# A two-block transformer on one core: tensor work moved across five attention seams, fewer convolution taps at a stage's end, and two norm factors taken at other strips

## The reference, cut to what matters

```
for l in range(2):                       # first block
    h = rms_norm(x, norm_g[l]);  proj = h @ w_in[l]
    q, k_c, v_c, k_s, v_s, k_w, v_w, g, z_nsa, u_lru, z_lru, glu_a, glu_b, z_conv = split(proj)
    y_nsa  = three attentions (compressed, selected, window), 8 heads, 2 kv heads, gated
    y_lru  = gated linear recurrence over a 4-tap convolution of u_lru
    y_conv = silu(layer_norm(dwconv31(glu_a * sigmoid(glu_b)))) @ w_pw2
    x = x + concat(y_nsa*silu(z_nsa), y_lru*silu(z_lru), y_conv*silu(z_conv)) @ w_out[l]
x = rms_norm(x, final_g)
for l in range(2):                       # second block
    h2 = rms_norm(x, ...)
    # l = 0: dense attention with normed and rotated heads, and window attention with a sink
    # l = 1: latent attention (w_uq, w_ukv), and neighbourhood attention on an 8 x 64 grid
    x = x + mixed @ w_out2
    m = rms_norm(mem, g_mem[l]);  k, v = split(m @ w_xkv[l])
    q = rms_norm(x, g3[l]) @ w_xq[l]
    x = x + cross_attention(q, k, v) @ w_xo[l]          # 4 heads of 128, 256 keys
    g, u = split(rms_norm(x, g4[l]) @ w_gate_up[l]);  x = x + (silu(g) * u) @ w_down[l]
out = rms_norm(x, final_g_2)
```

## Time and profile before

| | |
|---|---|
| median of 3 runs | 2329.72 us (2325.25 to 2330.05) |
| the profiled execution's own time | 2332.14 us |
| its span | 2330.3 us |
| PE busy | 2206.3 us, 95% |
| DVE / ACT / POOL busy | 1261.5 / 1088.9 / 867.2 us |
| mean granted TensorE clock | 0.976 of full |
| DMA | 187 MB, mean 80 GB/s |

### The profile page before, as it was taken

The page is one execution under the profiler, slowest core; times in us unless marked ns, Lnnn a source line. Parts: engine busy times, 40 slices in busy tenths (PEclk is TensorE's granted clock), DMA queues, the critical chain, the costliest instruction groups (busy, mean ns, idle before and its releaser), DMA issues.

```text
span 2330.3 us, 33123 instructions
## 1 busy us (share of the span) xinstructions
PE 2206.3 (95%) x12030; PEld 1783.9 (77%) x12030; DVE 1261.5 (54%) x2638; ACT 1088.9 (47%) x2178; POOL 867.2 (37%) x681
## 2 busy tenths in 40 slices
PE   7999889999989999889899999999879989999997
PEld 6788667887866788668788888888648878888886
DVE  5987782488778446885552112234677455221222
ACT  6642474564247542685453223333557545332332
POOL 4433204443330343004255555544130424554553
PEclk9999899999989999999999999999999999999999
DMA  4324003333400232003233333342110323333332
GB/s 160 90 90 141 15 2 86 100 91 90 138 22 6 87 96 73 28 12 101 66 96 95 96 108 99 94 129 74 41 44 28 92 81 87 100 93 101 96 94 69
DMA packets 105551, 186.96 MB, mean 80 GB/s; under 512 B 11440, under 2 KB 22704, under 8 KB 105264
## 3 DMA queue, kind: packets, MB, share of 16 engines
q1 hardware_dynamic: 99504, 175.91, 25.7%
q10 hardware_dynamic: 5888, 8.95, 1.2%
HBM read 182.71 MB, written 2.10 MB: 79 GB/s over the span
## 4 chain that ended last, share of the span: by engine, by line
PE 82%; DVE 11%; ACT 3%; issue 3%; POOL 1%; DMA 1%; SPq 0%; DVEq 0%; ACTq 0%
PE bank L801 22%; PE bank L803 22%; PE bank L802 22%; PE bank L1002 3%; PE bank L990 3%; PE bank L1015 3%; DVE temp L1816 2%; PE bank L910 1%; DVE temp L1848 1%; DVE bank L1932 1%; DVE op_lo L1464 1%; POOL w_lo L2100 1%; PE bank L862 1%; DVE temp L1850 1%; DVE conv_area L1473 1%
## 5 line engine op out<-in xcount | busy, mean ns | idle before, releaser
L2100 POOL TENSOR_TENSOR w_lo<-w_raw,w_hi 128x512 fp32r<-128x512 f32 (+2 forms) x620 | 821.1, 1330 | 1356.1 <-ACT w_hi L1120 1355.6
L801 PE MATMUL bank<-op_hi,w_hi 128*128 128x512 f32 x1840 | 733.4, 399 | 14.6 <-DVE op_lo L1464 9.5
L1120 ACT ACTIVATE w_hi<-w_raw 128x512 fp32r<-128x512 f32 (+2 forms) x636 | 385.8, 615 | 719.1 <-PE bank L803 714.3
L803 PE MATMUL bank<-op_hi,w_lo 128*128 128x512 f32 x1840 | 718.9, 391 | 0.0
L802 PE MATMUL bank<-op_lo,w_hi 128*128 128x512 f32 x1840 | 718.6, 391 | 0.0
L801 PEld LDWEIGHTS bank<-op_hi,w_hi 128*128 128x128 f32 x1840 | 346.8, 189 | 97.7 <-issue 12.0
L802 PEld LDWEIGHTS bank<-op_lo,w_hi 128*128 128x128 f32 x1840 | 347.0, 189 | 76.3 <-issue 5.7
L803 PEld LDWEIGHTS bank<-op_hi,w_lo 128*128 128x128 f32 x1840 | 346.5, 188 | 73.5
L1534 DVE TENSOR_TENSOR temp<-bank,rstd 128x512 f32<-128x512 f32 (+1 forms) x151 | 104.4, 691 | 410.7 <-PE bank L803 401.6
L801 PE MATMUL bank<-side_hi,w_hi 128*128 128x512 f32 (+2 forms) x632 | 238.8, 378 | 3.7 <-DVE side_lo L1464 2.9
L1603 DVE TENSOR_TENSOR x_t<-bank,x_t 128x512 f32<-128x512 f32 x80 | 55.3, 692 | 342.1 <-PE bank L803 342.0
(11 more groups left out here) (256 smaller groups left out, 2298.9 us busy)
## 6 DMA issues: line engine op xcount, KB each, us to landing
w_raw<-in_weights SPq DMA_DIRECT2D x618, 256.0 KB, 2.7
w_raw<-in_weights SPq DMA_DIRECT2D x34, 192.0 KB, 2.3
x_t<-in_x SPq DMA_DIRECT2D x8, 256.0 KB, 5.6
conv_area<-in_mem ACTq DMA_DIRECT2D x2, 1024.0 KB, 5.7
out_y<-ybuf SPq DMA_DIRECT2D x8, 256.0 KB, 2.1
conv_area<-in_bias ACTq DMA_DIRECT2D x1, 1920.0 KB, 7.9
conv_area<-in_bias ACTq DMA_DIRECT2D x2, 960.0 KB, 6.0
temp<-in_lru_w ACTq DMA_DIRECT2D x2, 512.0 KB, 8.9
```

Source lines behind the costliest of these rows:

```text
L801: pe.matmul(dst, w[0], m[0], start=start, stop=False)
L803: return pe.matmul(dst, w[1], m[0], start=False, stop=stop)
L1120: act.activation(w_hi[:, j, 0:m * w], w_raw[:, p % RAW_RING, 0:m * w], ACT.Copy).then_inc(*mark("weights_high", p))
L2100: pool.tensor_tensor(w_lo[:, j, 0:n], w_raw[:, p % RAW_RING, 0:n], w_hi[:, j, 0:n].bitcast(F32), ALU.subtract).then_inc(*mark("weights_spl ...
```

## The change

1. **Taps.** A's table has 8 more in all (the first glu_a strip 6 instead of 4, the three others 8 instead of 6), B's last two entries go from 6, 6 to 4, 0. The total is 124 as before.
2. **Order of AB.** Before: keys and queries of the rotated heads, those of the normed heads, then both value strips. Now kn, qn x4, v, kr, qr x4, v. `UNITS`, the list of the rotations, is sorted to suit.
3. **Factors.** Two chunks of the memory are split and squared with each of OUT2's first four strips. `mem` is summed in OUT2's strip 6 and spread before strip 7. `h3` is summed before the last strip of XV and spread before chunk 6 of the first XQ strip.
4. **Drain.** `strip` is a generator that yields after each chunk. `drain` issues chunks of the next part's first two strips inside the last four steps of an attention, by the table `DRAIN` (0 and 1 are the two strips; a tuple for each step, the fourth after the last values). Their first matmul also waits until DVE has read the scores that the bank held. ACT and DVE split the second strip's weights ahead too.

```diff
-TAPS = {"A": [0, 0, 0, 4, 5] + 3 * [1, 2, 6, 6, 4],
+TAPS = {"A": [0, 0, 0, 6, 5] + 3 * [1, 2, 6, 8, 4],
...
-            for m in (1, 0):
+            for m in range(2):
                 base = 768 * m
                 add(("AB", 0), "kn" if m == 0 else "kr", 0, "w_in_ab_2", 0, base + 512, DC, ("h2", l))
                 for c in range(4):
                     add(("AB", 0), "qn" if m == 0 else "qr", c, "w_in_ab_2", 0, base + P * c, DC, ("h2", l))
-            for m in range(2):
-                add(("AB", 0), "v", m, "w_in_ab_2", 0, 768 * m + 640, DC, ("h2", l))
+                add(("AB", 0), "v", m, "w_in_ab_2", 0, base + 640, DC, ("h2", l))
...
-        for s in STRIPS:
+        for s in sorted(STRIPS, key=lambda s: (s.n + 3, 1) if s.kind in ("qn", "kn") else (s.n + 1, 0)):
...
-            if part[0] == "XV":
-                FACTOR_STRIP[name] = (rng[1], 0), (rng[2], 6), rng[2]
-            elif part[0] == "XK" or part == ("A", 0):
+            if part[0] == "OUT2":
+                FACTOR_STRIP[name] = (rng[6], 0), (rng[7], 0), rng[6]
+            elif part[0] == "XQ":
+                FACTOR_STRIP[name] = (rng[0] - 1, 0), (rng[0], 6), rng[0]
+            elif part == ("A", 0):
...
+        DRAIN = {"NSA": ((), (), (0, 0), (0, 0, 1, 1, 1, 1)),
...
+                 "X2": ((), (), (0, 0, 1, 1), ())}
...
+            def strip(n, fresh, between, held=None):
+
                 s = STRIPS[n]
+                if held is not None:
+
+                    pe.wait_ge(*after("maxed", held))
...
-                    ins.then_inc(*mark("weights_used", p))
+                        if k == k0 + m - 1:
+                            ins.then_inc(*mark("weights_used", p))
+                        yield k
...
+            def drain(part, steps):
+
+                first = FOLLOWS[part]
+                for r in steps:
+                    n = first + r
+                    if n not in begun:
+                        held = [t["a"] for t in ATT[part] if t["bank"] == n % 2]
+                        begun[n] = strip(n, True, {}, held[-1])
+                    next(begun[n])
...
                         if s < len(pairs):
                             scores(pairs[s])
+                        if len(pairs) <= s < len(pairs) + 3:
+                            drain(part, steps[s - len(pairs)])
...
+                drain(part, steps[3])
...
-                        strip(n, STRIPS[n].operand not in seen, between)
+                        for _ in begun.pop(n, None) or strip(n, STRIPS[n].operand not in seen, between):
+                            pass
...
-                    if s.part[0] == "OUT2":
...
+                    if s.part[0] == "OUT2" and s.idx < DC // 2:
...
+                        for c in (2 * s.idx, 2 * s.idx + 1):
+                            high(("mem", l), c, mem_t[:, c, :], PR("g_mem", l, c))
+                            square(("mem", l), c, mem_t[:, c, :])
...
-                        split_to(last_of(FOLLOWS[part]))
+                        split_to(last_of(FOLLOWS[part] + 1))
```

More of the change, by code:

```diff
@@ L60 @@
 SUMS = 24
-TAPS = {"A": [0, 0, 0, 4, 5] + 3 * [1, 2, 6, 6, 4],
-        "B": [1, 0, 4, 3, 0, 5, 0, 0, 0, 2, 0, 6, 2, 6, 0, 3, 3, 5, 6, 6, 6]}
+TAPS = {"A": [0, 0, 0, 6, 5] + 3 * [1, 2, 6, 8, 4],
+        "B": [1, 0, 4, 3, 0, 5, 0, 0, 0, 2, 0, 6, 2, 6, 0, 3, 3, 5, 6, 4, 0]}
 COLS = dict(zip(
@@ L497, in build @@
         for l in range(LAYERS):
-            FACTOR.update({("A", l): ("h1", l), ("AB", 0) if l == 0 else ("DN", 0): ("h2", l), ("XK", l): ("mem", l),
-                           ("XV", l): ("h3", l), ("FF", l, 0): ("h4", l)})
+            FACTOR.update({("A", l): ("h1", l), ("AB", 0) if l == 0 else ("DN", 0): ("h2", l), ("OUT2", l): ("mem", l),
+                           ("XQ", l): ("h3", l), ("FF", l, 0): ("h4", l)})
         FACTOR_STRIP = {}
@@ L833, in first_spread @@
                 ins.then_inc(*mark("first_spread", 0))
-            def strip(n, fresh, between):
+            def strip(n, fresh, between, held=None):
                 s = STRIPS[n]
+                if held is not None:
+                    pe.wait_ge(*after("maxed", held))
                 if n >= 2:
@@ L958, in later @@
                     rotate(n)
+            begun = {}
+            def drain(part, steps):
[6 more added lines that the diff above has]
+                    next(begun[n])
             def attend(part):
                 ts, between = ATT[part], extras(part)
+                steps = DRAIN[part[0]]
                 def scores(pair):
@@ L1211, in evac @@
                     square(s.stat, s.idx, x_t[:, s.idx, :])
-                    if s.part[0] == "OUT2":
-                        l, c = s.part[1], s.idx
-                        if c == 0:
+                    if s.part[0] == "OUT2" and s.idx < DC // 2:
+                        l = s.part[1]
+                        if s.idx == 0:
                             act.wait_ge(*after("mem_in", l))
-                        high(("mem", l), c, mem_t[:, c, :], PR("g_mem", l, c))
-                        square(("mem", l), c, mem_t[:, c, :])
+                        for c in (2 * s.idx, 2 * s.idx + 1):
+                            high(("mem", l), c, mem_t[:, c, :], PR("g_mem", l, c))
+                            square(("mem", l), c, mem_t[:, c, :])
                 elif k == "cmp2" and s.idx == 0:
@@ L1673, in side @@
                     add_squares(s.stat, s.idx)
-                    if s.part[0] == "OUT2":
+                    if s.part[0] == "OUT2" and s.idx < DC // 2:
                         name = ("mem", s.part[1])
-                        low(name, s.idx, mem_t[:, s.idx, :], PR("g_mem", s.part[1], s.idx))
-                        add_squares(name, s.idx)
+                        for c in (2 * s.idx, 2 * s.idx + 1):
+                            low(name, c, mem_t[:, c, :], PR("g_mem", s.part[1], c))
+                            add_squares(name, c)
                 if n in TURNS:
```

11 lines of the change are left out of this document (6 added, 5 removed).

## The result

The changed kernel took 2316.24 us (median of 4 runs, 2313.19 to 2317.5), the kernel before 2329.12 beside it: a ratio of 0.9937 (95% interval 0.9923 to 0.9950), which is 14.7 us (12.9 between the medians). Built and run a second time it took 2318.82, a ratio of 0.9947 (0.9927 to 0.9968). The forecast was 2300 and a range of 2288 to 2312: the sign was right and half of the gain was missing.

What follows compares the result with a forecast made beforehand. PE was taken as the bound, busy 2206.3 of 2330.3 us. The terms sum to -29.8: 2332.1 profiled gives 2302.3, and the median, 2.4 lower, 2300. Own range 2296 to 2305; with the first three rivals 2288 to 2312.

Steps and rivals of the forecast that it cites:

- Taps: At both NSA starts PE begins 4.0 us earlier without trailing taps, -8.0; a wait in layer 0's A costs 1.2: -6.8.
- -1.5 for the clock behind the NSA starts: After the NSA starts, shorter idle should shorten PE's 11 us at clock 0.50: -1.5 in all, bounds 0 and -5.
- the 1.2 that I gave for A: In layer 0's A the added taps make PE wait for DVE once, +1.2 us, bounds 0 and 3.6.
- Factors: XK and XV take 26.5 us, 27.9 with costs moved elsewhere, in place of 35.8: -7.9 a layer, -15.8.
- The first rival: In XK and XV, DVE and POOL exclude each other wholly: 31.6 us a stage, 5.1 more each, 2310; chance 18%.
- my argument against it in the prediction: In XK and XV, at 1095.6 to 1101.6, PE was 5.97 of 6.00 us busy with DVE and POOL both at work.
- Order of AB: At AB2's start PE's idle falls from 6.8 to 4.0 us: -2.8, bounds -5.4 and +1 if DVE falls behind.
- Drains: Early chunks fill idle PE in attention tails: AB2 -1.8, C2 -0.9, D2 -0.5, NSA -2.3; X2 instead loses 2.6.
- +2.6 for X2: In the cross attentions' tails nothing covers the copy, high and low parts: +1.3 a layer, bounds -0.5 and +2.5 each.
- X2's +0.9 for the values behind twelve matmuls: In X2's tail the last values wait behind twelve matmuls, about 2.1 us idle follow, and strip 1 ends 0.9 later.
- The second rival: In the attention tails the drains bring nothing and only reorder; gains of 5.5 are gone: 2306; chance 12%.
- The fourth: Rival: the clock falls at XK's start and stays low, +12.4 a layer, 2357 if through XQ; chance 4%.

Runs made afterwards that it cites:

- k2: The kernel before with only the new taps and factors (old order of AB, no chunks in attentions, no early split): 2306.65 us, ratio 0.9893.
- j4: The changed kernel without any chunk inside an attention and without any early split of a second strip's weights: 2307.07 us, ratio 0.9901 to before.
- b1: The kernel before with the new table of taps alone: 2317.82 us, ratio 0.9958.
- b2: The kernel before with the memory's split, its factor and h3's factor at the new places alone: 2317.41 us, ratio 0.9948.
- e3: The changed kernel with the memory's split, its factor and that of h3 at their old places: 2332.39 us, ratio 1.0008 to before.
- b4: The kernel before with the new order of AB alone: 2330.26 us, ratio 1.0006.
- e2: The changed kernel with the old order of the AB strips and of the rotations: 2316.73 us, ratio 0.9944 to before.
- e4: The changed kernel without any chunk inside an attention, the second strip's weights still split ahead: 2312.95 us, ratio 0.9919 to before.
- b3: The kernel before with the chunks inside the attentions and the early split alone: 2341.44 us, ratio 1.0049.
- j2: The kernel before with chunks and early split of the second strip's weights in the two cross attentions (X2) alone: 2339.04 us, ratio 1.0037.

## Why the prediction was wrong, step by step

Medians: before 2330, taps and factors alone (k2) -24, with the new order of AB (j4) the same, with the chunks and the early split (the changed kernel) +9.

**Taps: right.** Forecast -6.8, and -1.5 for the clock behind the NSA starts; b1 measured -9.8 (ratio 0.9958, -6 to -14). Layer 0's start came at 247.92 where I had 247.1 and, with the 1.2 that I gave for A, 248.3. The clock behind them in 251 to 262 rose from 0.50 to 0.63:

```profile
251.00:262.00 11.00, 8.60 (x62) 6.40 (x61) 6.34 (x33) 7.36 (x26) 0.00 (x0) 0.63 0.01 1
```

**Factors: right.** -15.8 forecast; -12 by b2, -16 by e3, 14 by the matched stages. The stage is 25.3 us where I had 26.5, and what moved costs 2.2 elsewhere where I had 1.4. PE is the bound there now, busy in 25.00 of 25.30 us. That part of the mechanism was wrong: I had DVE as the bound, with 22.9 us of work, and it is busy for 17.77. The first rival's time (DVE and POOL exclude one another, 31.6) did not come:

```profile
L2130 POOL TENSOR_TENSOR w_lo<-w_raw,w_hi 128x512 fp32r<-128x512 f32 x9 | 13.7, 1525 | 11.9 <-ACT w_hi L1148 11.9
...
L1493 DVE SCALAR_TENSOR_TENSOR op_lo<-x_t,par,op_hi 128x512 fp32r<-128x512 f32 x7 | 6.3, 912 | 0.0
...
L1484 DVE TENSOR_TENSOR w_lo<-w_raw,w_hi 128x512 fp32r<-128x512 f32 x7 | 4.8, 692 | 0.4 <-ACT w_hi L1148 0.3
```

Its mechanism did, and my argument against it in the prediction was wrong. Five of the seven `w_lo` of DVE ran while POOL was idle, and the other two overlapped it by 0.39 and 0.15 us, so their 692 ns say little on the two together. An `op_lo` that starts inside a `w_lo` of POOL waits it out:

```profile
1093.35 2.44 DVE L1493 SCALAR_TENSOR_TENSOR op_lo<-x_t,par,op_hi 128x512 fp32r<-128x512 f32 x2
1093.46 1.78 POOL L2130 TENSOR_TENSOR w_lo<-w_raw,w_hi 128x512 fp32r<-128x512 f32 x1 [1.09 <-ACT w_hi L1148]
```

The first of the two `op_lo` began before POOL and took its usual 0.74, and POOL's 1.28 became 1.78. The second began at 1094.01, inside POOL's, took 1.78 and ended 0.55 us behind it. In the first traces of the two kernels 40 `op_lo` of this form began with more than 0.2 us of a `w_lo` of POOL ahead of them, and every one ended 0.55 us behind POOL's; instructions that read a PSUM bank, such as L1563, keep their 0.69 us beside POOL. The trace agrees with the contention that the Trainium skill gives for DVE instructions with two SBUF inputs ("GPSIMD Engine Reference", "1. Specifications"). The rival's 31.6 was too long because it added all of DVE's work to POOL's. In the stage DVE's instructions that read PSUM, 4.9 us, are not held up; the others, about 13 us undisturbed, and POOL's 11.5 fit into 25.3.

**Order of AB: wrong.** Forecast -2.8, measured 0 (b4 +1.4 with 3.5 either way; e2 against the changed kernel, k2 against j4: nothing). The step that failed is that DVE's work in the qn strips, put at 8.5 us for each strip against PE's 8.4, costs nothing; I had it only as a bound of +1. The start did win 2.6, but I counted DVE's work per strip and not where two kinds of rotation meet: `UNITS` puts the last normed rotation and the first rotated one into one strip, and PE, whose next matmul stands behind that rotation, waits 1.91.

**Drains: wrong, and the bulk of the miss.** Forecast -5.5 for four attentions and +2.6 for X2, -2.9 together (the 3.3 in the expectations of e4 and b3 is a wrong sum); measured +9 (2316.2 against j4's 2307.1). The step that failed is "A chunk issued early fills idle PE", priced from PE's idle time alone, with nothing for what the second strip's early weights do to the other engines. By the medians 3.3 of the 9 go with the chunks (e4) and 5.9 with the early split (e4 against j4), but the intervals of e4 and j4 overlap. Part of both is clock: the mean over the runs is 0.979 in the changed kernel and 0.981 in j4, and brought to one clock the 9 is about 5. In four points:
- The gain: in AB2 the chunks filled 0.77 of 1.03 us idle, and the switches between shapes and the wait for OUT2's first take-out took it back. Gain 0 in place of 1.8. In C2 and D2 nothing was gained that the stages could tell from the low clock.
- X2's +0.9 for the values behind twelve matmuls was right: the idle came, 1.90, and the third XO strip is 0.95 later than before (11.25 against 10.3 behind the last copy but one).
- The early split I costed at nothing, as part of the gain, and without a reason. It costs 1.0 in each X2 and gives 0.4 back, since POOL's second `w_lo` holds up a DVE instruction for which PE waits.
- The rest of X2's 3.2 and 4.1 is low clock: in the changed kernel it falls in 1136 to 1140, in the midst of the attention (the distance of the maxima is 1.5 longer), where before it fell on its start, under ACT's table load. j2 shows about the same sum, 3.2 to 3.4, with it in the tail in layer 0 and in the midst in layer 1. That the low clock moves there because of the early split or the chunks isn't shown.

**The second rival** (the drains bring nothing) pointed the right way with a price of 5.5, where 12 were due: "only reorder" left out what the early weights do to the other engines. The fourth, low clock through XK and XV, did not occur. The range was too narrow since the drains' bounds were taken from PE's idle time alone; for four of the attentions the slower bound was 0.

**Still open:** a part of b3. The chunks and the early split alone are 11.4 slower, while its profile's stages explain 3 for each X2 and little else. That profile is of its fastest execution (2336.50); four of the six took 2340.8 to 2342.9, at mean clocks of 0.974 to 0.976 against 0.978, and no trace shows where they lost it. Nor is it shown what decides where the clock falls.

## What to carry to other kernels

Work that is put into a gap of one engine is paid on all engines that prepare it: before moving it, ask what each of those instructions can hold up at that step (here POOL's `w_lo` held up a DVE instruction that PE waited for), and keep enough independent work behind the last dependent step to cover its chain. Where a wait at a barrier is removed (the taps) or a stage is freed of its factor steps, count on the gain; where PE is 95% busy and only reordered, count on none. Compare stages over several executions before believing 2 us in one.
